# A hybrid diffusion step: three quarters of four output panels move into the last attention group of the grouped-query layers, and GpSimd subtracts in four parts

## The chip, the cores and the metric

The kernel runs on one core of a Trainium2 chip. The metric is the device time of one execution in microseconds (us), the median of several runs. The engines are TensorE (PE, matmuls; PEld its weight loads), VectorE (DVE), ScalarE (ACT), GpSimd (POOL) and SyncE (SP, which here only issues DMA transfers). Each works through a queue of its own in order; semaphores tie them together.

## The reference, cut to what matters

Four layers run over 128 context and 512 latent tokens of width 1024. Layers 0 and 3 are grouped-query attention, layer 1 is differential attention, layer 2 an mLSTM. What the change touches is the end of a grouped-query layer, where the gated attention output is multiplied by `w_out` and added to the residual stream:

```
def gated_out(o, z, w_out):
    return (o.reshape(B, S, -1) * silu(z)) @ w_out

def layer(x, cond):                       # per layer
    shift, scale, gate = adaln(cond, w_mod, b_mod)
    h = rms_norm(x, norm_g) * (1 + scale) + shift
    q, k, v, z = split(h @ w_in)          # 16 query heads, 4 key/value heads
    o = softmax(q k^T / 8) v              # q, k normalised and rotated
    return x + gate * gated_out(o, z, w_out)
```

After layer 3 a last RMSNorm follows. All is float32.

## The kernel before, in words

Activations lie transposed, feature block by token: `x[p, block, token]`, eight blocks of 128 features (`KT`), 640 tokens. A float32 product is made of three passes in a faster format: weights and activations are each split into a high and a low part (`wh`, `wl`; `hh`, `hl` for the layer's input, `yh`, `yl` for the gated attention output), and a matmul unit runs high x high, high x low, low x high. One panel of 128 output features over all tokens is 8 x 3 x 2 = 48 matmuls of 128x128 by 320 tokens.

**Weights.** SP loads a panel of 256 KB into one of three slots of `raw` (in order, each slot when its last reader is done). POOL splits it in `split`: a 128x1 instruction, a cast into `wh`, a subtraction into `wl`, again three slots (`SPL`), each free when PE is done with the panel before. The modulation columns of the next layer (`mod_item`, `mods_at`) use the same `raw` slots; PE reads them directly.

**A grouped-query layer.** `gqa_layer` exists once for each engine. It runs 40 steps: four key/value heads (groups) of ten steps, two query blocks by five token tiles. A step n on PE is: wait for the exponentials of n, values of n - 1, scores of n + 1, transposes of n, and in between a half (320 tokens, 24 matmuls) of one projection panel of this or the next group, taken from a generator in two pieces. `unit_at(n)` says which half; in the last group only two of the ten steps have one (the z gate's second panel, steps 34 and 35). ACT takes exponentials and copies, DVE the maxima, the division and the gating product (`output`). A block b of `yh`, `yl` is complete after five steps: blocks 0 to 5 belong to the first three groups, 6 and 7 to the last.

**The output stretch.** `attention_out` then multiplies the eight panels of `w_out`, 48 matmuls each, into two PSUM accumulators in turn. DVE adds each to `x` with the layer's gate (`add_gated`) and sums its square (`squared`), for the next norm. The last panel (`last_panel`) runs half by half, and the sums of squares go through PE in between. In the last layer `turned_out` also transposes each finished block of `x` back to tokens, after ACT has scaled it; ACT copies the result out (`turned_read`).

The order on every engine is that of the written program; nothing is scheduled at run time.

## Time and profile before

| | |
|---|---|
| median of 3 runs | 2256.95 us (2256.05 to 2260.66) |
| the profiled execution | 2252.97 us, its span 2251.2 us |
| PE busy | 2058.2 us, 91% of the span |
| DVE, ACT, POOL busy | 1177.5, 803.4, 547.6 us (52, 36, 24%) |
| last group and output stretch of layer 3 | 2099.7 to 2175.5, and on to about 2237.6 us |
| last group of layer 0 | 332.7 to 416.2 us |

All times of the sections below are us from the span's start in the one profiled execution. A busy share is a mean over stages with different limits, so the stretches are looked at one by one. The granted clock is the share of TensorE's full speed: 1.00 is 2.4 GHz, 0.5 is 1.2 GHz, and a value between them is a mixture of both in time.

### The profile page before, as it was taken

The page shows a single profiled execution, that of the slowest core. Times are in us where ns is not written, and L with a number is a line of the kernel's source. Part 1 is how long each engine was busy: PE and PEld are TensorE (multiplying, and loading weights), DVE is VectorE, ACT ScalarE, POOL GpSimd, SP SyncE. Part 2 cuts the span into 40 slices and gives each one's busy share as a digit, 9 for nine tenths or more (in the row PEclk, how much of TensorE's full clock was granted, in tenths as well). Part 3 has the DMA queues.
Part 4 walks back from the last instruction along what each step waited for, and adds up shares of the span by engine and source line. Part 5 has one row for each costly group of instructions (what it writes and reads, how often), then busy time and mean ns, then how long its engine had stood idle before and what let it go on. Part 6 is the DMA issues. An engine that isn't in the chain of part 4 may idle for free.

```text
span 2251.2 us, 34991 instructions
## 1 busy us (share of the span) xinstructions
PE 2058.2 (91%) x14168; PEld 1765.2 (78%) x14168; DVE 1177.5 (52%) x2309; ACT 803.4 (36%) x1824; POOL 547.6 (24%) x440
## 2 busy tenths in 40 slices
PE   6999998889999997979979999998997989999888
PEld 4887886878989886968957868687876977888677
DVE  5477665563555553576534323241161666777544
ACT  5365554123444443031132232313221035555432
POOL 1313200433233311334310111102112542222122
PEclk8999998989999998979979999999998989999889
DMA  9212122322223223134222334325236221102001
GB/s 330 56 49 78 51 59 80 89 59 80 66 81 98 63 62 115 38 51 154 81 61 71 91 121 103 94 87 143 93 96 132 68 77 30 51 2 69 20 20 57
DMA packets 302286, 181.53 MB, mean 81 GB/s; under 512 B 59557, under 2 KB 276910, under 8 KB 302126
## 3 DMA queue, kind: packets, MB, share of 16 engines
q1 hardware_dynamic: 283860, 158.39, 24.0%
q10 hardware_dynamic: 18266, 20.90, 4.1%
q8 instruction: 113, 1.85, 0.4%
q14 instruction: 47, 0.39, 0.1%
HBM read 153.51 MB, written 25.74 MB: 80 GB/s over the span
## 4 chain that ended last, share of the span: by engine, by line
PE 75%; DVE 9%; ACT 8%; DMA 3%; issue 3%; SPq 1%; ACTq 1%; POOL 0%; DVEq 0%; POOLq 0%
PE pc L1682 20%; PE acc L1608 12%; PE acc L710 5%; PE acc L1774 4%; PE acc L1763 4%; PE pt L1785 3%; PE acc L700 3%; PE pc L765 3%; PE pt L710 2%; PE acc L1992 2%; PE acc L2004 2%; DMA out_mlstm_n<-amat 1%; PE acc L654 1%; PE pt L2012 1%; PE acc L1938 1%
## 5 line engine op out<-in xcount | busy, mean ns | idle before, releaser
L1523 POOL TENSOR_TENSOR idle<-eps 128x1 f32<-128x1 f32 x144 | 38.1, 264 | 1637.8 <-PE pc L765 306.0
L1682 PE MATMUL pc<-hh,wh 128*128 128x320 f32 x1152 | 380.0, 330 | 16.7 <-DVE hl L2661 8.2
L1526 POOL TENSOR_TENSOR wl<-raw,wh 128x1024 fp32r<-128x1024 f32 x144 | 368.0, 2556 | 11.5
L1682 PE MATMUL pc<-hl,wh 128*128 128x320 f32 x1152 | 362.1, 314 | 0.0
L1682 PE MATMUL pc<-hh,wl 128*128 128x320 f32 x1152 | 361.9, 314 | 0.0
L1682 PEld LDWEIGHTS pc<-hh,wh 128*128 128x128 f32 x1152 | 221.8, 192 | 29.0 <-issue 15.7
L1682 PEld LDWEIGHTS pc<-hl,wh 128*128 128x128 f32 x1152 | 222.8, 193 | 0.2 <-issue 0.2
L1682 PEld LDWEIGHTS pc<-hh,wl 128*128 128x128 f32 x1152 | 221.9, 193 | 0.0
L2283 ACT COPY ht<-pt 128x512 f32<-128x512 f32 (+1 forms) x160 | 76.4, 525 | 214.8 <-PE pt L1785 214.6
L1524 POOL CAST wh<-raw 128x1024 fp32r<-128x1024 f32 x144 | 150.9, 1048 | 0.0
L1774 PE MATMUL acc<-ht,gvt 128*64 128x128 f32 x1344 | 100.7, 298 | 19.3 <-ACT ht L2288 14.9
L1774 PEld LDWEIGHTS acc<-ht,gvt 128*64 128x64 f32 x1344 | 80.2, 148 | 45.6 <-issue 24.7
L2756 DVE TENSOR_REDUCE gst<-acc 128x1 f32<-128x640 f32 (+1 forms) x160 | 113.3, 708 | 3.0 <-PE acc L1763 2.8
L2746 DVE TENSOR_TENSOR gyt<-acc,gzs 128x128 f32<-128x128 f32 x80 | 23.1, 289 | 175.2 <-PE acc L1763 164.0
L2951 DVE SCALAR_TENSOR_TENSOR x<-acc,mod,x 128x128 f32<-128x128 f32 x72 | 36.3, 546 | 139.2 <-PE acc L1608 127.1
L1763 PE MATMUL acc<-gkk,gqf 64*128 64x320 f32 (+1 forms) x576 | 103.3, 476 | 6.1 <-ACT two L2274 6.1
L1608 PE MATMUL acc<-hh,wh 128*128 128x320 f32 x368 | 87.4, 319 | 18.2 <-POOL wl L1526 13.1
L1608 PE MATMUL acc<-yh,wh 128*128 128x320 f32 x400 | 92.1, 311 | 0.0
L1608 PE MATMUL acc<-yl,wh 128*128 128x320 f32 x400 | 91.7, 310 | 0.0
L1608 PE MATMUL acc<-yh,wl 128*128 128x320 f32 x400 | 91.6, 310 | 0.0
L1608 PE MATMUL acc<-hl,wh 128*128 128x320 f32 x368 | 85.7, 315 | 0.0
L1608 PE MATMUL acc<-hh,wl 128*128 128x320 f32 x368 | 85.4, 314 | 0.0
(386 smaller groups left out, 4437.6 us busy)
## 6 DMA issues: line engine op xcount, KB each, us to landing
raw<-in_w_mod SPq DMA_DIRECT2D x144, 256.0 KB, 3.4
raw<-in_gqa_w_in SPq DMA_DIRECT2D x80, 256.0 KB, 3.6
raw<-in_diff_w_in SPq DMA_DIRECT2D x64, 256.0 KB, 3.8
raw<-in_mlstm_w_in SPq DMA_DIRECT2D x64, 256.0 KB, 3.4
praw<-in_w_mod SPq DMA_DIRECT2D x32, 256.0 KB, 9.9
raw<-in_gqa_w_out SPq DMA_DIRECT2D x32, 256.0 KB, 3.2
out_mlstm_C<-amat ACTq DMA_DIRECT2D x16, 512.0 KB, 7.4
raw<-in_mlstm_w_out SPq DMA_DIRECT2D x32, 256.0 KB, 3.1
```

The costliest lines, as they stand in the source:

```text
L700: ins = pe.matmul(acc[b][:, 0:r[1] - r[0]], mk[:, kt, i * P:(i + 1) * P], mq[:, kt, r[0]:r[1]], start=kt == 0, stop=kt == 3)
L710: return pe.matmul(dst, lhsT, rhs, start=start, stop=stop, skip_group_check=True)
L765: ins = pe.matmul(pc[:, c:c + 320], w[:, blk % 2, kt, :], h[:, kt, t:t + 320], start=kt == 0 and n == 0, stop=kt == KT - 1 and n == 2)
L1524: pool.tensor_copy(wh[:, s], raw[:, r]).then_inc(pool_step, 1)
L1526: pool.tensor_tensor(wl[:, s], raw[:, r], wh[:, s].bitcast(F32), ALU.subtract).then_inc(w_full[s], 1)
L1608: ins = pe.matmul(acc[b][:, c:c + 320], w[:, s, kt, :], h[:, kt, t:t + 320], start=kt == 0 and n == 0, stop=kt == KT - 1 and n == 2)
L1682: ins = pe.matmul(pc[:, c:c + 320], w[:, sl, kt, :], h[:, kt, t:t + 320], start=kt == 0 and n == 0, stop=kt == KT - 1 and n == 2)
L1763: ins = pe.matmul(acc[j][:, o:o + c1 - c0], gqf[r, g % 2, blk, q], gkk[r, g % 2, c0:c1], start=True, stop=True)
L1774: ins = pe.matmul(acc[0][HD * j:HD * j + HD, 0:P], gvt[:, g % 2, t, :], ht[:, j, i * P:(i + 1) * P], start=i == 0, stop=t == tiles[-1], sk ...
L1785: ins = pe.transpose(pt[:, 512 * j + i * P:512 * j + (i + 1) * P], gee[n % 2][:, j, i * P:(i + 1) * P], ident)
L2283: act.copy(ht[:, j, 0:w], pt[:, 512 * j:512 * j + w]).then_inc(pts_dve, 1)
L2756: step(dve.tensor_reduce(gst[:, p, j:j + 1], acc[j][:, AO:AO + w], AX.X, ALU.max, negate=True))
```

## The change

- `unit_at`: in the last group the z gate's second panel moves from steps 34, 35 to steps 30, 31.
- `early_at`, `early_mms`: steps 32 to 39 each take half of one of the output panels 0 to 3, but only over the six row blocks that exist by then (`EARLY_KT`): 18 matmuls into `pc`, in two pieces of 9. DVE adds the half to `x` one step later (`early_gated`).
- `attention_out`: panel 4 comes first, then one panel of weights that holds the last two row blocks for panels 0 to 3, 12 matmuls each, then panels 5, 6, 7. In the last layer the transposes follow that order, three in a row behind panel 5 and two behind panel 6.
- SP and POOL load and split the panels in that order. A grouped-query layer now has nine panels of output weights instead of eight, so the slots of layer 1 begin elsewhere (`FIRST_SLOT`).
- `split`: the subtraction is made in four instructions of 256 elements instead of one of 1024, for all 144 (now 146) splits of the kernel.

```diff
@@ -389,9 +390,23 @@
         def unit_at(n):
 
             g, s = n // NS2, n % NS2
+            if g == GQ_KV - 1:
+                return ("z1", g, s) if s < 2 else None
             kind = KINDS[s // 2]
             grp = g + (kind != "z1")
             return (kind, grp, s % 2) if grp < GQ_KV else None
+
+        def early_at(n):
+
+            s = n - (GQ_KV - 1) * NS2 - 2
+            return (s // 2, s % 2) if s >= 0 else None
+
+        def out_slots(kind, layer):
+
+            s = FIRST_SLOT[layer] + PANELS[kind]
+            if kind == "diff":
+                return [((s + i) % SPL, (i,)) for i in range(KT)]
+            return [((s + EARLY + i) % SPL, panels) for i, panels in enumerate(GQ_OUT)]
 
         def mods_at(n, layer):
...
@@ -409,7 +424,10 @@
 
         FIRST = ("kv", "q0", "q1", "z0")
         PANELS = {"gqa": 5 * GQ_KV, "diff": 4 * NH}
-        FIRST_SLOT = (0, 1, 0, 2)
+        FIRST_SLOT = (0, 2, 0, 2)
+        EARLY, EARLY_KT = 4, 6
+        GQ_OUT = ((4,), (0, 1, 2, 3), (5,), (6,), (7,))
+        LAST_ORDER = [i for panels in GQ_OUT for i in panels]
 
         def totals(kind, layer):
...
@@ -1449,8 +1467,16 @@
                             item(at[0], at[1])
                             if at[0] == "q0":
                                 cache(at[1])
-                        if n >= NN - 2:
-                            whole(ring(), wo, (n - NN + 2) * P, [w_full[wring()]] * RAW)
+                        early = early_at(n)
+                        if early is not None and early[1] == 0:
+                            whole(ring(), wo, early[0] * P, [w_full[wring()]] * RAW)
+                        if n == NN - 2:
+                            whole(ring(), wo, EARLY * P, [w_full[wring()]] * RAW)
+                        if n == NN - 1:
+                            slot = ring()
+                            panel(slot, [(raw[:, slot, 4 * k:4 * k + 4, :],
+                                          wo[(EARLY_KT + k) * P:(EARLY_KT + k + 1) * P, 0:EARLY * P].rearrange("p (i c) -> p i c", c=P))
+                                         for k in range(2)], [w_full[wring()]] * RAW)
                         for m in mods_at(n, layer):
                             mod_item(m)
...
@@ -1523,8 +1549,10 @@
                 pool.tensor_tensor(idle[:, :], eps[:, 0:1], eps[:, 0:1], ALU.add)
                 pool.tensor_copy(wh[:, s], raw[:, r]).then_inc(pool_step, 1)
                 pool.wait_ge(*seen(pool_step))
-                pool.tensor_tensor(wl[:, s], raw[:, r], wh[:, s].bitcast(F32), ALU.subtract).then_inc(w_full[s], 1)
-                seen.lend(("w", s), done[s])
+                for k in range(0, KT, 2):
+                    ins = pool.tensor_tensor(wl[:, s, k:k + 2], raw[:, r, k:k + 2], wh[:, s, k:k + 2].bitcast(F32), ALU.subtract)
+                ins.then_inc(w_full[s], 1)
+                seen.lend(("w", s), done[s], times)
 
             pool.wait_ge(x_in, QT)
...
@@ -1546,8 +1574,11 @@
                         at = unit_at(n)
                         if at is not None and at[2] == 0:
                             split(ring(), wring(), units)
+                        early = early_at(n)
+                        if early is not None and early[1] == 0:
+                            split(ring(), wring(), [early_done] * SPL, 2)
                         if n >= NN - 2:
-                            split(ring(), wring())
+                            split(ring(), wring(), proj_done, 1 if n == NN - 2 else EARLY)
                         for m in mods_at(n, layer):
                             mod_item()
...
@@ -1697,6 +1728,36 @@
 
                 seen(raw_full[ring()], 32)
                 outs_open.append(wring())
+
+            def early_mms(half):
+
+                sl, (t, c) = early_slot[0], HALF[half]
+                seen.back(pe, ("c", half))
+                for kt in range(EARLY_KT):
+                    for n, (w, y) in enumerate(((wh, yh), (wh, yl), (wl, yh))):
+                        ins = pe.matmul(pc[:, c:c + 320], w[:, sl, kt, :], y[:, kt, t:t + 320],
+                                        start=kt == 0 and n == 0, stop=kt == EARLY_KT - 1 and n == 2)
+                        if kt == EARLY_KT // 2 - 1 and n == 2:
+                            yield
+                ins.then_inc(early_done, 1)
+                seen.lend(("c", half), early_added)
+
+            def early_panel(n, gen):
+
+                early = early_at(n)
+                if early is None:
+                    return None
+                if gen is None:
+                    if early[1] == 0:
+                        seen(raw_full[ring()], 32)
+                        early_slot[0] = wring()
+                        pe.wait_ge(*seen(w_full[early_slot[0]]))
+                        pe.wait_ge(*seen.at(y_ready, EARLY_KT))
+                    gen = early_mms(early[1])
+                    next(gen)
+                    return gen
+                for _ in gen:
+                    pass
 
             def mod_sum(m, at):
...
@@ -1885,10 +1946,11 @@
                     if n + 1 < NN:
                         scores(n + 1)
                     turn_p(n)
-                    gen = part(n, None)
+                    gen, early = part(n, None), early_panel(n, None)
                     if n % QT:
                         turn_fifth(n)
                     part(n, gen) if gen else None
+                    early_panel(n, early) if early else None
                     if st == 1:
                         rotate_q("q1", g)
...
@@ -1924,7 +1986,8 @@
                 seen.end(totals(kinds[layer], layer))
                 if turn.k % 2 == 0:
                     turn()
-                for i in range(2, KT):
+                final = layer + 1 == DEPTH
+                for i in range(2 if kinds[layer] == "diff" else EARLY + 1, KT):
                     out_panel()
                 first = outs_open[0]
                 pe.wait_ge(*seen(w_full[first]))
-                    pe.wait_ge(fin_full, kt + 1)
-                    if kt >= 2:
-                        pe.wait_ge(fin_read, kt - 1)
+                if kinds[layer] == "diff":
+                    for sl in outs_open[1:-1]:
+                        project(sl, yh, yl, freed_by=x_ready)
+                    last_panel(outs_open[-1], yh, yl)
+                    outs_open.clear()
+                    return
+
+                def turned_out(p):
+
+                    dst = (pt, pc)[p % 2]
+                    pe.wait_ge(fin_full, p + 1)
+                    if p >= 2:
+                        pe.wait_ge(fin_read, p - 1)
                     for q in range(QT):
-                        ins = pe.transpose(dst[:, q * P:(q + 1) * P], ht[:, kt % 2, q * P:(q + 1) * P], ident)
+                        ins = pe.transpose(dst[:, q * P:(q + 1) * P], ht[:, p % 2, q * P:(q + 1) * P], ident)
                     ins.then_inc(fin_turned, 1)
 
-                final = layer + 1 == DEPTH
-                for i, sl in enumerate(outs_open[1:-1]):
+                for half in range(2):
+                    seen.back(pe, ("c", half))
+                rest = outs_open[1]
+                pe.wait_ge(*seen(w_full[rest]))
+                for i in range(EARLY):
+                    b = buffer(x_ready)
+                    for kt in range(KT - EARLY_KT):
+                        for n, (w, y) in enumerate(((wh, yh), (wh, yl), (wl, yh))):
+                            for t, c in halves():
+                                ins = pe.matmul(acc[b][:, c:c + 320], w[:, rest, 4 * kt + i, :], y[:, EARLY_KT + kt, t:t + 320],
+                                                start=kt == 0 and n == 0, stop=kt == KT - EARLY_KT - 1 and n == 2)
+                    ins.then_inc(proj_done[rest], 1)
+                if final:
+                    turned_out(0)
+                for k, sl in enumerate(outs_open[2:-1]):
                     project(sl, yh, yl, freed_by=x_ready)
                     if final:
-                        turned_out(i)
+                        for p in ((1, 2, 3), (4, 5))[k]:
+                            turned_out(p)
                 bs = last_panel(outs_open[-1], yh, yl, final)
...
@@ -2703,6 +2788,15 @@
                     dve.wait_ge(*seen(zt_ready))
                     dve.scalar_tensor_tensor(out=gzs[:, int(kind == "z1"), t:t + 320], in0=gzt[:, t:t + 320], scalar=1.0, in1=pc[:, c:c + 320],
                                              op0=ALU.add, op1=ALU.mult).then_inc(c_free[half], 1)
+
+                def early_gated(i, half):
+
+                    (t, c), mod = HALF[half], mods[layer % 2]
+                    dve.wait_ge(*seen(early_done))
+                    for a0, a1, g in (((0, P, 0), (P, 320, 1)), ((0, 320, 1),))[half]:
+                        ins = dve.scalar_tensor_tensor(out=x[:, i, t + a0:t + a1], in0=pc[:, c + a0:c + a1], scalar=mod[:, 2 * KT + i, g:g + 1],
+                                                       in1=x[:, i, t + a0:t + a1], op0=ALU.mult, op1=ALU.add)
+                    ins.then_inc(early_added, 1)
 
                 def k_reciprocal(j):
...
@@ -2799,7 +2893,11 @@
                         output(n - 1)
                     at = unit_at(n - 1) if n else None
                     if at is not None and at[0] in ("z0", "z1"):
+                        if not more and at[0] == "z1":
+                            dve.wait_ge(*seen.at(o_ready, NS2 * g))
                         gate(*at)
+                    if n and early_at(n - 1) is not None:
+                        early_gated(*early_at(n - 1))
                     if st == 1 and g:
                         y_low(2 * g - 1)
                     if st == 2:
@@ -2826,6 +2924,7 @@
                 if layer + 1 < DEPTH:
                     modulation(layer + 1)
                 y_low(NN // QT - 1)
+                early_gated(*early_at(NN - 1))
                 seen.end(totals("gqa", layer))
                 if turn.k % 2 == 0:
...
@@ -2999,11 +3098,17 @@
                 else:
                     diff_layer()
 
-                for i in range(KT - 1):
-                    add_gated((FIRST_SLOT[layer] + PANELS[kind] + i) % SPL, i, layer)
-                    dve.wait_ge(*seen(x_ready))
-                    squared(i)
-                last_gated((FIRST_SLOT[layer] + PANELS[kind] + KT - 1) % SPL, layer)
+                if kind == "gqa":
+                    dve.wait_ge(*seen(early_added, 2 * EARLY))
+                outs, p = out_slots(kind, layer), 0
+                for s, panels in outs[:-1]:
+                    for i in panels:
+                        add_gated(s, i, layer)
+                    for i in panels:
+                        dve.wait_ge(*seen(x_ready))
+                        squared(i, p)
+                        p += 1
+                last_gated(outs[-1][0], layer)
             use()
             dve.wait_ge(*seen(root_ready))
```

PE in the last group of layer 3, from the values matmuls behind the short tile on (`ht`, `gvt`: values; `gkk`, `gqf`: scores; `two`, `gee`: transposes of the probabilities; `yh`, `yl`, `wh`, `wl`: output panels). Before:

```order
L1774 MATMUL acc<-ht,gvt 64x128 x2
L1763 MATMUL acc<-gkk,gqf 128x320 x4
L1785 MATMUL pt<-consts,two 128x128 x8
L1794 MATMUL pt<-consts,two 128x128 x2
L1774 MATMUL acc<-ht,gvt 64x128 x10
```

And of the change, up to the first three of the 18 early matmuls of that step:

```order
L1835 MATMUL acc<-ht,gvt 64x128 x2
L1824 MATMUL acc<-gkk,gqf 128x320 x4
L1846 MATMUL pt<-consts,two 128x128 x8
L1738 MATMUL pc<-yh,wh 128x320
L1738 MATMUL pc<-yl,wh 128x320
L1738 MATMUL pc<-yh,wl 128x320
```

Where the step had only attention, nine output matmuls now stand ahead of the fifth tile's transposes and nine behind them.

SP's queue in the last group of layer 0 (`in_w_mod`: modulation columns, two rows for each; `in_gqa_w_out`: output panels, two rows each). Before:

```order
L1384 DMA raw<-in_gqa_w_in 128x4x128 x2
L1384 DMA raw<-in_w_mod 128x4x128 x12
L1384 DMA raw<-in_gqa_w_out 128x4x128 x2
L1384 DMA raw<-in_w_mod 128x4x128 x2
L1384 DMA raw<-in_gqa_w_out 128x4x128 x2
L1384 DMA raw<-in_w_mod 128x4x128 x2
L1384 DMA raw<-in_gqa_w_out 128x4x128 x12
```

And of the change, from the second pair of columns of the group on:

```order
L1402 DMA raw<-in_w_mod 128x4x128 x4
L1402 DMA raw<-in_gqa_w_out 128x4x128 x2
L1402 DMA raw<-in_w_mod 128x4x128 x4
L1402 DMA raw<-in_gqa_w_out 128x4x128 x2
L1402 DMA raw<-in_w_mod 128x4x128 x4
L1402 DMA raw<-in_gqa_w_out 128x4x128 x2
L1402 DMA raw<-in_w_mod 128x4x128 x8
L1402 DMA raw<-in_gqa_w_out 128x4x128 x4
L1402 DMA raw<-in_w_mod 128x4x128 x2
L1402 DMA raw<-in_gqa_w_out 128x512 x2
L1402 DMA raw<-in_w_mod 128x4x128 x2
L1402 DMA raw<-in_gqa_w_out 128x4x128 x6
```

Output panels now stand between the columns instead of behind nearly all of them, and the row of 128x512 is the panel of the last two row blocks.

DVE in one step of the last group of layer 3 (`gst`: maxima and their scaling, `gee`: the division, `yl`: low part of a finished block). Before:

```order
L2746 TENSOR_TENSOR gyt<-acc,gzs 128x128
L2756 TENSOR_REDUCE gst<-acc 128x1
L2757 TENSOR_TENSOR gst<-gst,grq 128x1
L2691 TENSOR_TENSOR yl<-gyt,yh 128x640
L2765 RECIPROCAL gst<-gst 128x1
L2766 SCALAR_TENSOR_TENSOR gee<-gee,gst,half_col 128x640
```

And of the change:

```order
L2840 TENSOR_TENSOR gyt<-acc,gzs 128x128
L2850 TENSOR_REDUCE gst<-acc 128x1
L2851 TENSOR_TENSOR gst<-gst,grq 128x1
L2797 SCALAR_TENSOR_TENSOR x<-pc,mod,x 128x320
L2776 TENSOR_TENSOR yl<-gyt,yh 128x640
L2859 RECIPROCAL gst<-gst 128x1
```

The addition of an early half (`x<-pc,mod,x`) stands behind the step's maxima and ahead of the division.

## Rows read from the trace of the kernel before

**Rows 1.** The page, busy us of each engine, share of the span, instructions.

```profile
PE 2058.2 (91%) x14168; PEld 1765.2 (78%) x14168; DVE 1177.5 (52%) x2309; ACT 803.4 (36%) x1824; POOL 547.6 (24%) x440
```

**Rows 2.** Busy time by stretch: third and last groups of layers 0 and 3.

```profile
core 0: us, PE busy (x) PEld busy (x) DVE busy (x) ACT busy (x) POOL busy (x), PEclk, DMA share, GB/s
253.10:332.70 79.60, 78.13 (x678) 65.99 (x674) 56.91 (x110) 44.85 (x104) 14.85 (x12) 1.00 0.22 62
332.70:416.20 83.50, 65.77 (x602) 49.96 (x598) 44.00 (x91) 35.45 (x83) 12.81 (x11) 0.82 0.33 95
2024.00:2099.70 75.70, 74.57 (x601) 63.34 (x600) 55.89 (x110) 44.08 (x100) 20.75 (x15) 1.00 0.20 59
2099.70:2175.50 75.80, 56.92 (x381) 41.73 (x381) 40.55 (x91) 32.76 (x72) 7.40 (x6) 0.80 0.05 15
```

**Rows 3.** The chain that ended last, layer 3's output stretch: start, us, what.

```profile
2191.11 0.55 PE pt L1948 x5
2191.65 7.05 PE acc L1608 x48
```

**Rows 4.** DVE's timeline in that stretch, additions: start, us, instruction, idle before.

```profile
2184.10 1.01 DVE L2951 SCALAR_TENSOR_TENSOR x<-acc,mod,x 128x128 f32<-128x128 f32 x2 [5.33 <-PE acc L1938]
...
2233.17 0.68 DVE L2977 SCALAR_TENSOR_TENSOR x<-acc,mod,x 128x128 f32<-128x128 f32 x2 [1.27 <-PE acc L1636]
```

**Rows 5.** ACT's timeline in that stretch, the scaling of one block.

```profile
2230.21 0.83 ACT L2521 ACTIVATE ht<-x,cols 128x640 f32<-128x640 f32 x1 [6.18 <-DVE x L2951]
```

**Rows 6.** Busy time by step: 20, 21, 22, 24, 28 and 29 of layer 3.

```profile
2024.00:2030.40 6.40, 6.40 (x55) 5.45 (x54) 3.61 (x10) 3.37 (x8) 0.00 (x0) 1.00 0.41 111
2030.40:2038.00 7.60, 7.48 (x49) 5.75 (x48) 6.45 (x11) 4.74 (x12) 4.60 (x5) 1.00 0.67 196
2038.00:2047.50 9.50, 9.50 (x77) 7.96 (x76) 6.94 (x13) 5.12 (x10) 3.19 (x2) 1.00 0.19 57
...
2055.40:2063.70 8.30, 8.28 (x70) 7.51 (x70) 8.09 (x14) 4.68 (x11) 4.23 (x3) 1.00 0.22 65
...
2086.00:2093.30 7.30, 7.30 (x64) 6.32 (x63) 5.35 (x11) 4.71 (x10) 4.00 (x3) 1.00 0.24 72
2093.30:2099.70 6.40, 6.40 (x59) 5.93 (x58) 3.03 (x11) 2.77 (x8) 0.00 (x0) 1.00 0.01 3
```

**Rows 7.** PE's timeline, step 22 of layer 3: the key sums.

```profile
2046.35 1.29 PE L1807 MATMUL pt<-gsk,consts 64*64 64x320 f32 x4
```

**Rows 8.** ACT's timeline, steps 32 and 33 of layer 3.

```profile
2121.70 1.28 ACT L2301 ACT_TABLE_LOAD   x1
...
2126.64 1.07 ACT L2283 COPY ht<-pt 128x512 f32<-128x512 f32 x2 [3.37 <-PE pt L1785]
```

**Rows 9.** Timeline of a step at clock 1.00 (35 of layer 3): PE, then ACT.

```profile
2140.19 1.31 PE L1774 MATMUL acc<-ht,gvt 128*64 128x128 f32 x20
2141.44 1.35 PE L1763 MATMUL acc<-gkk,gqf 64*128 64x320 f32 x8
...
2144.99 0.88 ACT L2274 ACTIVATE two<-acc,gst,grq 128x640 f32<-128x640 f32 x1
```

**Rows 10.** SP's and POOL's timeline in layer 0, from a panel's issue to its split.

```profile
391.04 1.06 SPq L1384 DMA_DIRECT2D raw<-in_gqa_w_out  x2
...
395.55 0.19 POOL L1523 TENSOR_TENSOR idle<-eps 128x1 f32<-128x1 f32 x1 [45.67 <-DMA raw<-in_gqa_w_out]
...
396.80 2.36 POOL L1526 TENSOR_TENSOR wl<-raw,wh 128x1024 fp32r<-128x1024 f32 x1
```

**Rows 11.** Timeline of POOL, DVE and PE: layer 3's step 24, layer 0's output stretch.

```profile
2056.86 2.85 POOL L1526 TENSOR_TENSOR wl<-raw,wh 128x1024 fp32r<-128x1024 f32 x1
2057.89 1.84 DVE L2757 TENSOR_TENSOR gst<-gst,grq 128x1 f32<-128x1 f32 x1
...
469.23 2.88 DVE L2962 TENSOR_TENSOR two<-two 128x640 f32<-128x640 f32 x1
...
472.26 1.04 PE L1650 MATMUL acc<-two,consts 128*128 128x320 f32 x3 [1.54 <-DVE two L2962]
```

**Rows 12.** The page's groups: matmuls of the mLSTM's output, idle before and releaser.

```profile
L1608 PE MATMUL acc<-hh,wh 128*128 128x320 f32 x368 | 87.4, 319 | 18.2 <-POOL wl L1526 13.1
```

44 lines of the change are left out of this document (22 added, 22 removed).

## The prediction

> **What bounds the kernel now.** The page comes first: TensorE (PE) is busy for 91% of the span and no other engine is near it [rows 1], so time is won by taking PE's instructions off the path, by filling PE's idle time, or by raising its clock. The second view is the busy time by stretch. It shows a difference inside the attention of a grouped-query layer. An ordinary group of ten steps (steps 20 to 29; ten steps per key/value head) takes 79.6 us in layer 0 and 75.7 us in layer 3, PE busy for 78.1 and 74.6 us, granted clock 1.00. The last group (steps 30 to 39) has 192 fewer projection matmuls and takes 83.5 and 75.8 us: PE is busy for only 65.8 and 56.9 us, and the granted clock is 0.82 and 0.80 [rows 2]. A clock of 0.80 between the levels 2.4 and 1.2 GHz means 40% of the stretch at the lower one. So the last group does less and takes as long: it idles, and the idling brings slow matmuls. Third, the chain that ended last: right behind that group stand eight output panels, 48 matmuls each, 7.05 us per panel with nothing between them but 0.55 us of transposes in the last layer [rows 3]. That stretch is pure PE. The change moves work from the full stretch into the hollow one.
>
> **The output stretch.** Of panels 0 to 3, six of eight row blocks go into steps 32 to 39: 4 x 36 = 144 matmuls per layer. The rest, 4 x 12, costs what one panel did. At 7.05/48 = 0.147 us a matmul [rows 3] the stretch loses 21.1 us, for two layers **-42.2**.
>
> The four short accumulations of the rest panel (12 x 0.147 = 1.76 us each) alternate between two accumulators, and each wants VectorE's (DVE's) addition of the one two back: one takes 1.01 us [rows 4], so DVE keeps up. Four squares are queued behind these additions instead of between them. They have one panel of PE time (7 us) and are needed two panels later; nothing waits. In the last layer three transposed panels stand in a row behind panel 5, through two buffers. The third waits for ScalarE (ACT) to copy out the first (about as long as its scaling of one panel, 0.83 us [rows 5]) and to scale the next: 0.55 + 0.8 + 0.8 - 1.1 = **+1.0**, once.
>
> **The last group.** What one step costs I read from ordinary steps with their 24 projection matmuls, all at clock 1.00 [rows 6], and take off what is missing: 6 x 0.147 = 0.88 us where 18 early matmuls stand for 24.
> - 30 and 31 (the z1 panel moved here): 6.4 and 7.6, as steps 20 and 21.
> - 32: step 22 (9.5) less the next head's key sums (1.2 [rows 7]) less 0.88: 7.4.
> - 33: ACT loads a table and takes one root while PE still works on values (1.25), scores (1.3) and half of the transposes (0.4); then it copies (1.07), loads the other table (1.28) and takes two exponentials (1.9): 6.9, with the semaphores between some 7.2 [rows 8, 9]. PE, with 6.4, waits here.
> - 34: step 29 (6.4) less 0.88: 5.5.
> - 35: PE would need 5.5, but from the start of the values matmuls over scores and maxima to the end of the second exponential, which the next step waits for, are 5.7 (2140.19 to 2145.87) [rows 9]: the floor of any full step.
> - 36: step 28 (7.3) less 0.88, less 16 of 20 values matmuls (1.0): 5.4.
> - 37, 38: 7.3 - 0.88 = 6.4 each. 39: without scores (1.3), 5.1.
>
> Sum 63.1. DVE gets the additions of the early halves, 0.68 us where a half has two pieces and less where it has one [rows 4], behind its maxima, while ACT takes exponentials; the transposes want DVE's result only 2.5 us (values and scores) into the next step, so PE's other matmuls hide them. Six weight splits of GpSimd (POOL) fall in this group and can hold up DVE inside the floor chain: +1.0. Layer 3: 64.1 against 75.8, **-11.7**. The bounds: 63 below, and above the 75.7 of an ordinary group, if something other than PE sets the length of its steps. I take the lower end because PE was busy for 74.6 of those 75.7 us.
>
> Layer 0 also has 12 sums of modulation columns in this group. Four of them lengthen its ordinary group by 79.6 - 75.7 = 3.9 us, so 0.98 each: 63.1 + 1.0 + 11.7 = 75.8. Here the transfer queue (SP's) matters: early panels and columns share three landing slots, and SP issues in order. From an issue to POOL's start are 4.5 us, from there to the subtraction 1.25, the subtraction takes 2.36 and its added parts 0.6: together 8.7 [rows 10]. Panel 3 gets its slot when the second column of step 36 has been copied, about 1.8 us into step 37 counting the issue ahead of it, and is ready at 10.5; PE wants it at 7.4 + 3.4 = 10.8. Column 23 follows the split of panel 4: ready 0.4 + 8.7 + 4.5 = 13.6 us into step 38, wanted at 7.4 + 5.2. I allow 1.5: 77.3 against 83.5, **-6.2**. In layer 3 there are no columns and weights come two steps early.
>
> **The subtraction in parts.** A DVE instruction that reads SBUF twice can stand still until POOL's subtraction ends: a product of two 128x1 columns took 1.84 us and ended at 2059.73, the subtraction beside it at 2059.71. In layer 0's output stretch a sum of squares took 2.88 in that way, and PE waited 1.54 us for it [rows 11]. A quarter of 2.36 is 0.6, and that wait shrinks to some 0.4: **-1.1**. Elsewhere PE's idle time in the six ordinary groups is about 1.1 to 1.5 each, 8 in all [rows 2], half of it the table loads of step 23; I take **-2.0**, bounds 0 and -4. The price: three more instructions per split, at most 0.19 each, what a 128x1 one takes [rows 10]. It is hidden wherever weights are early; in the mLSTM's output stretch PE waited 13.1 us for one split [rows 12], so **+0.6** there.
>
> The Trainium skill (GPSIMD Engine Reference, section 3.1 Elementwise) speaks against parts: each instruction pays two software dispatch hops and a join of eight cores. Its 4497 ns for 2048 elements at 2.6 cycles leave, as an estimate, 0.06 us for that, or +0.2 for my +0.6.
>
> **Sum.** -42.2 + 1.0 - 11.7 - 6.2 - 1.1 - 2.0 + 0.6 = -61.6. The durations are those of the profiled execution, 2252.97 us (span 2251.2), which becomes 2191.4; it lies 4.0 below the median of the runs, so against 2256.95 I forecast **2195**.
>
> **Rivals.**
> *The last group keeps an ordinary group's length.* If the additions on DVE, or stalls behind POOL, hold each step at what it took with 24 matmuls, the groups take 75.7 and 79.6 + 8 x 0.98 = 87.4: +3.8 in place of -17.9, so -39.9, **2217**. For it: DVE is busy for 8.1 of 8.3 us in step 24, and POOL splits more often here. Against it: that step's length was PE's, and the last group has no rotation or key scaling for a next head. Chance 0.17.
>
> *Weights late in layer 0.* If panels 3, 4 and the rest each come a whole 8.7 us late, 26 us go again: **2221**. For it: three slots, an in-order queue, and a margin of 0.3 us worked out above. Against it: the lateness would have to add up from panel to panel, while each step leaves 7 us. Chance 0.07.
>
> *The clock falls in the last group: slower.* Place: steps 32 to 39. Their PE work at the upper level is some 47 us per layer and doubles at the lower: +94 for both layers against -61.6 gives +32, **2289**. It decides from two thirds of those steps at 1.2 GHz on. For it: this very group ran 40% of its time there. Against it: it idled 19 of 76 us, and the ordinary groups of [rows 2] have 1.00 at 98% busy; the new steps idle only in 33 and 35, about 1 us. The Trainium skill (TensorE: Matmul & The Clock Gate, section A second HAM failure mode: psum-queue depth-cycling) has such a case: matmul groups that rotate through PSUM banks leave short idle times, and the clock swings. Ordinary steps rotate through the same two halves of pc each step and show no fall, so here row and rule differ. Chance 0.03.
>
> **How the numbers follow.** The forecast, with its unknowns (group sums within 6, parts from 0 to -4, lateness 0 to 5), holds 2184 to 2206 and has 0.73. A measurement tells 0.2% (4.5 us) from no change. The range goes down to 2183 and up over the first rival's value to **2218**, which leaves out about 0.05 below and 0.1 above. Only the clock case is on the other side: faster 0.96, same 0.01, slower 0.03.
>
> **What would show it.** Right: the last groups at 62 to 67 and 73 to 80 us with clock near 1.00; the output stretch from the last values to the end of the last panel shorter by 21 us per layer; one PE wait of 1 us before the third transposed panel; DVE's slowest 128x1 product under 0.9 us. Wrong: PE idle in steps 34 to 38 with DVE as the releaser (first rival), PE waiting for wl or raw in layer 0 (second), clock 0.5 in steps 32 to 39 (third).

## The result and the profile after

The changed kernel takes **2180.09 us** (median of 4 runs, 2179.51 to 2181.97) beside 2258.71 us (2256.05 to 2260.66) for the kernel before on the same chip: a ratio of 0.9657, 95% interval 0.9643 to 0.9671. The forecast was 2195 us and its range began at 2183: the direction was right, but the gain, 78 us, is larger than forecast, and the time lies 2.9 us under the range.

The page's busy time, the line that answers to [rows 1]:

```profile
PE 2021.1 (93%) x14168; PEld 1742.8 (80%) x14168; DVE 1114.4 (51%) x2333; ACT 803.8 (37%) x1824; POOL 653.9 (30%) x884
```

PE has as many matmuls as before and needs 37 us less for them. POOL is busy for 106 us more, and DVE, with 24 instructions more, for 63 us less. Nothing in the change takes work from DVE. So DVE records must contain time in which the instruction stood still, and that time fell.

The last groups, by stretch (layer 0, then layer 3), which answer to the second and fourth row of [rows 2]:

```profile
core 0: us, PE busy (x) PEld busy (x) DVE busy (x) ACT busy (x) POOL busy (x), PEclk, DMA share, GB/s
333.97:409.84 75.87, 72.19 (x748) 61.02 (x740) 47.77 (x102) 35.58 (x84) 27.05 (x37) 1.00 0.44 126
2057.78:2122.63 64.85, 62.70 (x526) 53.24 (x524) 45.92 (x102) 32.77 (x72) 22.69 (x30) 1.00 0.14 42
```

83.5 became 75.9 and 75.8 became 64.9, with more matmuls in them and the clock at 1.00 instead of 0.82 and 0.80. The same view by step, layer 3, steps 30 to 39 in order:

```profile
2057.78:2064.18 6.40, 6.40 (x56) 5.45 (x54) 3.57 (x8) 2.84 (x8) 3.98 (x6) 1.00 0.14 40
2064.18:2071.44 7.26, 7.26 (x50) 5.73 (x48) 6.42 (x14) 4.41 (x10) 0.53 (x2) 1.00 0.14 39
2071.44:2078.85 7.41, 7.41 (x67) 6.54 (x66) 5.24 (x11) 4.07 (x8) 3.71 (x5) 1.00 0.25 73
2078.85:2086.70 7.85, 6.59 (x58) 5.54 (x57) 4.97 (x13) 5.03 (x10) 1.11 (x2) 1.00 0.00 0
2086.70:2092.27 5.57, 5.46 (x52) 5.10 (x52) 4.60 (x13) 2.34 (x7) 3.90 (x5) 1.00 0.06 18
2092.27:2098.10 5.83, 5.70 (x50) 4.58 (x48) 3.00 (x9) 2.29 (x7) 0.00 (x0) 1.00 0.26 75
2098.10:2104.43 6.33, 5.79 (x40) 4.55 (x40) 6.19 (x11) 4.05 (x9) 4.91 (x6) 1.00 0.02 7
2104.43:2110.87 6.44, 6.33 (x56) 5.48 (x56) 4.71 (x13) 3.08 (x7) 0.00 (x0) 1.00 0.26 77
2110.87:2117.35 6.48, 6.48 (x58) 5.48 (x56) 4.62 (x12) 3.12 (x7) 4.55 (x6) 1.00 0.04 13
2117.35:2122.63 5.28, 5.28 (x49) 4.78 (x48) 2.62 (x6) 1.53 (x3) 0.00 (x0) 1.00 0.30 86
```

The forecast for these steps was 6.4, 7.6, 7.4, 7.2, 5.5, 5.7, 5.4, 6.4, 6.4, 5.1. It missed step 33 by 0.65 and step 36 by 0.9 us; in step 36 PE stood still for 0.54 us, DVE was busy for 6.19 of the 6.33 us and POOL was splitting for 4.91.

PE's timeline in the output stretch of layer 3, the transposes behind panel 5:

```profile
2145.75 0.71 PE L2018 MATMUL pc<-consts,ht 128*128 128x128 f32 x5
2146.30 0.71 PE L2018 MATMUL pt<-consts,ht 128*128 128x128 f32 x5
2147.97 0.77 PE L2018 MATMUL pc<-consts,ht 128*128 128x128 f32 x5 [0.96 <-ACT ht L2606]
```

The third one waits 0.96 us for ACT; 1.0 was forecast.

The instruction whose stall [rows 11] showed, all 160 of it in the kernel before and in the changed one (shortest, median and longest in ns):

```profile
L2757 DVE TENSOR_TENSOR gst<-gst,grq x160: 158/159/2315, 91.7 to 2168.1; 128x1 f32<-128x1 f32 x160
L2851 DVE TENSOR_TENSOR gst<-gst,grq x160: 159/160/750, 95.0 to 2115.9; 128x1 f32<-128x1 f32 x160
```

The longest is 0.75 us, under the 0.9 forecast. Before, it was 2.32 us; the one that [rows 11] showed, 1.84 us, was not the longest.

### The profile page after: what moved, and what is told of

The parts are those of the page before. It is cut to its first block, busy times and chain, and to the rows that moved or that the text cites. A ratio compares the mean times of both kernels' runs of the same rounds, so it can differ in the third digit from the quotient of the medians.

```text
span 2178.5 us, 35475 instructions
## 1 busy us (share of the span) xinstructions
PE 2021.1 (93%) x14168; PEld 1742.8 (80%) x14168; DVE 1114.4 (51%) x2333; ACT 803.8 (37%) x1824; POOL 653.9 (30%) x884
## 4 chain that ended last, share of the span: by engine, by line
PE 77%; DVE 8%; ACT 7%; DMA 4%; issue 2%; SPq 1%; ACTq 1%; POOL 0%; DVEq 0%; POOLq 0%
PE pc L1713 21%; PE acc L1639 10%; PE acc L728 6%; PE acc L1835 4%; PE acc L1824 4%; PE pc L783 3%; PE acc L718 3%; PE pt L1846 3%; PE pt L728 3%; PE acc L2076 2%; PE acc L2088 2%; DMA out_mlstm_n<-amat 1%; PE acc L672 1%; PE acc L1667 1%; PE pt L2096 1%
## 5 line engine op out<-in xcount | busy, mean ns | idle before, releaser
L1549 POOL TENSOR_TENSOR idle<-eps 128x1 f32<-128x1 f32 x146 | 43.5, 298 | 1458.8 <-PE pc L783 297.5
L1553 POOL TENSOR_TENSOR wl<-raw,wh 128x256 fp32r<-128x256 f32 x584 | 467.2, 831 | 11.7
L1713 PE MATMUL pc<-hh,wh 128*128 128x320 f32 x1152 | 381.0, 331 | 15.8 <-DVE hl L2743 7.7
L1639 PE MATMUL acc<-hh,wh 128*128 128x320 f32 x368 | 86.9, 318 | 18.7 <-POOL wl L1553 13.2
L1824 PE MATMUL acc<-gkk,gqf 64*128 64x320 f32 (+1 forms) x576 | 95.4, 445 | 4.7 <-ACT two L2358 4.7
L1835 PE MATMUL acc<-ht,gvt 128*64 128x128 f32 x1344 | 91.0, 278 | 3.8 <-ACT ht L2372 3.4
L1835 PEld LDWEIGHTS acc<-ht,gvt 128*64 128x64 f32 x1344 | 71.9, 136 | 28.1 <-issue 22.4
L783 PE MATMUL pc<-hh,wh 128*128 128x320 f32 x256 | 81.2, 317 | 1.0 <-issue 0.7
L728 PE MATMUL acc<-mv,amat 128*128 128x256 f32 (+1 forms) x344 | 80.7, 380 | 0.0
L1639 PEld LDWEIGHTS acc<-hh,wh 128*128 128x128 f32 x368 | 62.7, 192 | 20.8 <-issue 13.4
```

What stands on the lines that cost most here:

```text
L728: return pe.matmul(dst, lhsT, rhs, start=start, stop=stop, skip_group_check=True)
L783: ins = pe.matmul(pc[:, c:c + 320], w[:, blk % 2, kt, :], h[:, kt, t:t + 320], start=kt == 0 and n == 0, stop=kt == KT - 1 and n == 2)
L1553: ins = pool.tensor_tensor(wl[:, s, k:k + 2], raw[:, r, k:k + 2], wh[:, s, k:k + 2].bitcast(F32), ALU.subtract)
L1639: ins = pe.matmul(acc[b][:, c:c + 320], w[:, s, kt, :], h[:, kt, t:t + 320], start=kt == 0 and n == 0, stop=kt == KT - 1 and n == 2)
L1713: ins = pe.matmul(pc[:, c:c + 320], w[:, sl, kt, :], h[:, kt, t:t + 320], start=kt == 0 and n == 0, stop=kt == KT - 1 and n == 2)
L1824: ins = pe.matmul(acc[j][:, o:o + c1 - c0], gqf[r, g % 2, blk, q], gkk[r, g % 2, c0:c1], start=True, stop=True)
```

## Where the time went, stretch by stretch

Lengths in us, from the start of one matmul to the start of another in each kernel's profiled execution: a grouped-query layer's groups from the values matmuls of step 0 to those of 29 and of 39; its output from there to the first matmul of the last panel; the convolution from the first gate matmul of the mLSTM to the end of its last convolution addition on DVE. The columns in the middle are experiments told below.

| stretch | before | before + 4 parts | changed, 1 part | changed | changed, again |
|---|---|---|---|---|---|
| start, to layer 0's values | 99.4 | 99.7 | 100.4 | 104.3 | 98.0 |
| layer 0, groups 0 to 2 | 233.3 | 229.3 | 233.6 | 229.8 | 229.6 |
| layer 0, last group | 83.5 | 82.4 | 78.4 | 75.9 | 75.4 |
| layer 0, output | 50.85 | 50.85 | 29.96 | 29.74 | 29.74 |
| layer 0, last panel | 9.75 | 8.11 | 12.40 | 8.19 | 8.16 |
| mLSTM, convolution | 174.5 | 170.0 | 173.0 | 167.5 | 167.5 |
| mLSTM, what follows to its last panel | 673.3 | 676.8 | 680.2 | 670.2 | 680.9 |
| ahead of layer 3 | 61.8 | 59.5 | 61.8 | 59.6 | 59.4 |
| layer 3, groups 0 to 2 | 220.3 | 219.6 | 220.4 | 219.6 | 219.6 |
| layer 3, last group | 75.8 | 72.0 | 67.1 | 64.9 | 64.8 |
| layer 3, output | 53.85 | 53.84 | 33.89 | 33.89 | 33.88 |

Three things are in it. The outputs are shorter by 21.1 and 20.0 us and the last groups by 7.6 and 10.9, near the forecast. The parts gain in stretches that the forecast gave nothing or little. And two stretches, the start and the mLSTM behind its convolution, differ by 6.3 and 10.7 us between two executions of the same changed kernel; a difference in them says nothing about the change. Layer 0's last group also varies: in two other profiles whose layer 0 is the kernel before it took 79.8 and 85.5 us, so its 7.6 us could as well be 4 or 10. Layer 3's took 75.4 to 75.8 us in the same three profiles.

## The experiments

The theory after the result: what was mis-sized is the subtraction in parts. By this theory, any DVE instruction that reads SBUF twice stands still for one GpSimd instruction on a panel, so stalls shrink with the length of that instruction, in every stretch where DVE is on the path. The rival: the parts are worth the 2.5 us of the forecast, and the rest came from the slots or from the filled steps.

### The parts alone, the early panels alone, the slots alone

Before with the four parts (shortened):

```diff
-wl[:, s], raw[:, r], wh[:, s] in one subtraction
+for k in range(0, KT, 2): wl[:, s, k:k + 2], raw[:, r, k:k + 2], wh[:, s, k:k + 2]
```

> The kernel before with the subtraction in four parts and nothing else. If the parts are what shortened the mLSTM layer (theory): that layer about 10 us shorter than before between the end of layer 1 and its own last panel, ordinary groups of the grouped-query layers 4 us shorter together, norms and tails 4 us; ratio to before 0.991 to 0.994 (14 to 20 us). If the shifted weight slots did it (rival): the mLSTM layer as before, ratio 0.996 to 0.999.

The changed kernel with the subtraction whole (the same edit backwards):

> The changed kernel with the subtraction whole again; early panels, moved z gate and order of the output kept. Theory: the moved panels alone give 53 to 59 us as the terms of the prediction have it (output stretches 41 us, last groups 11 and 7): 2195 to 2205 us, mLSTM layer as long as before. Rival (slots): mLSTM layer still 10 us shorter, 2185 us or less.

Before with the slots of the change:

```diff
-        FIRST_SLOT = (0, 1, 0, 2)
+        FIRST_SLOT = (0, 2, 0, 2)
```

> The kernel before with the slots of layer 1, and so those that the mLSTM layer finds free first, shifted as in the changed kernel, and nothing else. Theory: within 0.1% of before. Rival: 8 to 10 us shorter, all of it in the mLSTM layer.

| kernel | median us (range) | ratio to before, 95% interval |
|---|---|---|
| before + 4 parts | 2241.54 (2239.51 to 2244.35) | 0.9922 (0.9904 to 0.9940) |
| changed, subtraction whole | 2210.44 (2208.55 to 2212.04) | 0.9780 (0.9765 to 0.9795) |
| before, other slots | 2260.3 (2254.95 to 2266.66) | 1.0001 (0.9986 to 1.0015) |

The parts alone bring 17.7 us (0.0078 x 2261.6), not 2.5. The rest of the change alone brings 49.8 us, less than the 53 to 59 expected. On top of it the parts bring some 28 us more by the two ratios (0.9780 and 0.9657), or 25 with the changed kernel run again (0.9667, below). The slots make no difference that can be told from none (interval 3 us either way). The rival is out. One expectation failed: with the parts alone the mLSTM layer was to be 10 us shorter; its convolution is 4.5 us shorter, but what follows is 3.5 us longer, which is within what that stretch varies by.

### Which length counts

The changed kernel with the subtraction in two and in eight instructions:

```diff
-                for k in range(0, KT, 2):    # 256 elements each
+                for k in range(0, KT, 4):    # the first kernel: 512
+                for k in range(0, KT, 1):    # the second: 128
```

> The changed kernel with the subtraction in two instructions of 512 elements instead of four. With one instruction it took 2210.4 us, with four 2180.1 us. Theory (what is saved goes with the length of one instruction, which other engines must sit out: 2.56 us whole, 0.83 us as a quarter, some 1.4 us as a half): two thirds of the 30 us come back at once, 2188 to 2193 us. Rival (only the breaking up as such counts, a wait of 1.4 us is as harmless as one of 0.8): 2178 to 2183 us.

> The changed kernel with the subtraction in eight instructions of 128 elements. Theory (length of one instruction, here some 0.5 us): another 5 us, 2173 to 2177 us. Rival (each further instruction costs GpSimd about 0.25 us, as the step from one to four did, 2.56 to 3.32 us per split, and where TensorE waits for the split that shows): 2181 to 2186 us.

| parts | mean of one, us | all subtractions, POOL us | DVE busy, us | median us (range) |
|---|---|---|---|---|
| 1 | 2.55 | 372 | 1193.6 | 2210.44 (2208.55 to 2212.04) |
| 2 | 1.41 | 407 | 1150.1 | 2189.87 (2188.37 to 2190.57) |
| 4 | 0.83 | 467 | 1114.4 | 2180.09 (2179.51 to 2181.97) |
| 8 | 0.53 | 574 | 1084.5 | 2177.51 (2172.86 to 2183.31) |

Two parts came out at 2189.9 inside the theory's 2188 to 2193. From one part to four POOL is busy for 95 us more and DVE for 79 us less, and down to four parts the time follows the length of one instruction. At eight the range of the runs covers both sides: a gain of 2.6 us is not told from none, and the ratios to before are the same (0.9657 and 0.9661). The rule does not hold in every place. With one, two, four and eight parts the convolution takes 173.0, 170.6, 167.5 and 166.9 us, but the last panel of layer 0 takes 12.4, 12.5, 8.2 and 8.5: there halves are no better than the whole.

### Where the stalls are

Parts in the mLSTM layer alone, then in layers 0 and 3 alone, on the kernel before (shortened):

```diff
+            def split(r, s=None, done=proj_done, parts=1):    # 4 from mlstm_pool
+            parts = 4 if kind == "gqa" else 1                 # the second kernel
```

> The kernel before with the subtraction in four parts in the mLSTM layer alone (48 of 144 splits). In all layers it brought 17.7 us. Theory (VectorE's column additions in the mLSTM's convolution are the path there, and stand still for a whole subtraction): 5 to 9 us of it are here, 2252 to 2257 us, the four heads' convolution phase about 169 us instead of 174.5. Rival 1 (all of it is won in the attention layers, what the mLSTM shows is the spread of its transfers): 2260 to 2263 us. Rival 2 (all of it is here): 2242 to 2246 us.

> The kernel before with the subtraction in four parts in layers 0 and 3 alone. In all layers it brought 17.7 us, in the mLSTM layer alone 5 to 7. Theory (the grouped-query layers hold the rest: steps that stand still for a subtraction and then run at a lower granted clock, the last panel of layer 0, the last groups): 10 to 13 us, 2246 to 2249 us, and no step of layer 0's ordinary groups above 9.7 us. Rival (the forecast was right here, 2.0 + 1.1 us, and the rest is in the differential layer): 2254 to 2257 us.

The mLSTM alone: 2251.41 us (2248.53 to 2258.93), ratio 0.9977 (0.9960 to 0.9994), some 5 us, with a convolution of 170.0 us. Layers 0 and 3 alone: 2244.29 us (2232.97 to 2249.85), ratio 0.9933 (0.9908 to 0.9959), some 15 us. No step of layer 0's ordinary groups is above 9.7 us there any more. The first gain is at the low end of the 5 to 9 us expected, the second above its 10 to 13. The two add up to the 17.7 within their intervals, so nothing points to the differential layer, which was not tried alone. The convolution took 172.1 to 174.6 us in the five profiles that have the subtraction whole there, and 167.5 to 170.0 in the five with four parts and the cast whole. With parts only in layers 0 and 3, the last panel of layer 0 stays at 9.75 us: the subtraction beside it is that of a panel of layer 1.

Three places show how a stall becomes PE's time. First the last panel of layer 0, POOL, DVE and PE in the changed kernel with the subtraction whole:

```profile
433.18 0.82 DVE L3058 TENSOR_TENSOR two<-x 128x640 f32<-128x640 f32 x1
435.71 1.03 POOL L1550 CAST wh<-raw 128x1024 fp32r<-128x1024 f32 x1
435.75 1.67 DVE L3059 TENSOR_TENSOR two<-two 128x640 f32<-128x640 f32 x1
436.83 2.87 POOL L1552 TENSOR_TENSOR wl<-raw,wh 128x1024 fp32r<-128x1024 f32 x1
437.46 2.92 DVE L3058 TENSOR_TENSOR two<-x 128x640 f32<-128x640 f32 x1
...
444.25 2.83 POOL L1552 TENSOR_TENSOR wl<-raw,wh 128x1024 fp32r<-128x1024 f32 x1
444.89 1.01 DVE L3048 SCALAR_TENSOR_TENSOR x<-acc,mod,x 128x128 f32<-128x128 f32 x2
...
448.78 2.47 PE L1679 MATMUL acc<-two,consts 128*128 128x320 f32 x4 [2.64 <-DVE two L3059]
```

and in the changed kernel:

```profile
434.86 4.46 POOL L1553 TENSOR_TENSOR wl<-raw,wh 128x256 fp32r<-128x256 f32 x4
435.49 1.25 DVE L3061 TENSOR_TENSOR two<-two 128x640 f32<-128x640 f32 x1
...
443.34 1.31 PE L1681 MATMUL acc<-two,consts 128*128 128x320 f32 x4
```

A square takes 0.82 us by itself, 2.92 beside the whole subtraction and 1.25 beside a quarter. The addition that reads PSUM and `x` is not held up (1.01 us beside a subtraction, as in [rows 4]). PE waits 2.64 us for the sum of squares, or not at all.

The mLSTM's convolution, DVE and POOL, with the subtraction whole:

```profile
993.01 5.59 DVE L1168 SCALAR_TENSOR_TENSOR cv<-r,cols,cv 128x642 f32<-128x642 f32 x3
995.03 2.87 POOL L1552 TENSOR_TENSOR wl<-raw,wh 128x1024 fp32r<-128x1024 f32 x1
```

and in the changed kernel:

```profile
984.09 3.94 DVE L1168 SCALAR_TENSOR_TENSOR cv<-r,cols,cv 128x642 f32<-128x642 f32 x3
986.14 4.73 POOL L1553 TENSOR_TENSOR wl<-raw,wh 128x256 fp32r<-128x256 f32 x4
```

Three additions take 1.65 us less; the phase repeats such places for each of four heads and is 4.5 to 7 us shorter with parts.

The third goes through the clock. Steps 2 and 3 of layer 0, first with the subtraction whole (the run with other slots), then in the changed kernel:

```profile
109.20:120.51 11.31, 10.69 (x78) 8.15 (x76) 7.70 (x12) 5.92 (x12) 5.37 (x4) 0.90 0.01 1
120.51:131.13 10.62, 10.21 (x82) 8.16 (x82) 5.77 (x11) 5.87 (x13) 0.00 (x0) 0.78 0.00 0
```

```profile
111.88:121.40 9.52, 9.52 (x77) 7.97 (x76) 7.07 (x12) 5.29 (x11) 7.53 (x10) 1.00 0.01 3
121.40:129.73 8.33, 7.93 (x79) 6.70 (x78) 5.43 (x10) 6.21 (x14) 0.00 (x0) 1.00 0.00 0
```

In the first pair, this is what happened in step 2: the subtraction, the product of two columns that stands still, and ACT, which waits for it:

```profile
112.24 2.40 POOL L1526 TENSOR_TENSOR wl<-raw,wh 128x1024 fp32r<-128x1024 f32 x1
112.66 2.00 DVE L2757 TENSOR_TENSOR gst<-gst,grq 128x1 f32<-128x1 f32 x1
...
114.69 0.89 ACT L2274 ACTIVATE gee<-acc,gst,grq 128x640 f32<-128x640 f32 x1 [1.43 <-DVE gst L2757]
```

PE idled 0.6 us later in that step (the profile names no releaser, so that this stall is the reason is argued from the order). The granted clock was 0.90 over that step and 0.78 over the next, and the two steps together took 4.1 us longer. In the profile of the kernel before, step 13, behind such a stall, ran at 0.83 and took 9.9 us instead of 8.3; in four others with the subtraction whole it was step 3 or 23 or both. With four parts, steps 2, 12 and 22 take 9.5 us and steps 3, 13 and 23 8.33 in every profile. So in layer 0 the parts save the stall and the slow matmuls behind it, together 4 to 7 us in the ordinary groups. Not every such stall is followed by slow matmuls (step 12 of the same run was not), and what decides it was not tried.

### What made the last group short

> The changed kernel, with only two of the six row blocks multiplied in steps 32 to 39 (6 matmuls a step instead of 18); four row blocks of panels 0 to 3 are left out of the output. Theory (the last group was long because PE idled and its clock fell): with less to do the last group of layer 3 is no shorter than the 64.9 us of the changed kernel, granted clock 0.8 to 0.9, group 66 to 74 us. Rival (the clock does not matter, only PE's own work and the chain of maxima and exponentials): 96 matmuls less make it 55 to 60 us.

```diff
-                for kt in range(EARLY_KT):
+                for kt in range(2):
...
```

This kernel leaves out four of six row blocks of the early panels and was run once. Steps 33 and 35 of layer 3, then its whole last group:

```profile
2085.84:2093.69 7.85, 4.74 (x46) 3.68 (x47) 5.92 (x15) 5.84 (x10) 2.94 (x5) 1.00 0.00 1
2098.42:2104.65 6.23, 3.84 (x38) 2.82 (x39) 3.71 (x10) 2.49 (x7) 2.22 (x4) 1.00 0.08 25
...
2065.73:2127.91 62.18, 50.23 (x431) 40.21 (x431) 45.31 (x102) 32.34 (x72) 23.50 (x31) 0.97 0.14 43
```

62.2 us, between what the theory and the rival expected, so neither is right as put. Twelve of 18 matmuls less shorten the group by only 2.7 us (step 33 not at all): the steps stand near a floor, which the prediction took for the chain from values over maxima to exponentials. Step 33 stays at 7.85 us, as the ordinary step 23 with 24 matmuls does. With 6 matmuls per step the granted clock was 0.97, where the old group had 0.80. The full 18 therefore cost almost nothing there. In layer 0 the same kernel's last group even took 77.3 us at a clock of 0.96, longer than the 75.9 with all 18.

Then one move of the change alone, on the kernel before:

```diff
+            if g == GQ_KV - 1:
+                return ("z1", g, s) if s < 2 else None
...
+                        if not more and at[0] == "z1":
+                            dve.wait_ge(*seen.at(o_ready, NS2 * g))
```

> The kernel before with one thing of the change: the second panel of the z gate in the last group stands in its first two steps instead of its fifth and sixth. No early panels, the subtraction whole. Theory (the last group is short in the changed kernel because its steps are filled and the clock stays up): the empty steps leave the granted clock below 0.9, the last groups keep 70 us or more in layer 3 and 78 or more in layer 0, the time is within 6 us of before, 2255 to 2262. Rival (the last groups were long because of where the z gate's panel stood): 62 to 67 us in layer 3, and 2238 to 2248 us in all.

The last groups of layers 0 and 3:

```profile
336.04:422.08 86.04, 69.90 (x600) 52.57 (x599) 43.33 (x91) 35.42 (x84) 9.66 (x9) 0.76 0.32 93
2107.77:2174.70 66.93, 49.91 (x382) 37.73 (x382) 39.35 (x91) 32.34 (x72) 7.33 (x6) 0.88 0.06 17
```

2248.57 us (2241.41 to 2254.72), ratio 0.9961 (0.9943 to 0.9980): some 9 us are gained, more than the theory allowed and just less than the rival's 10 to 20. In layer 3 the rival is right about the group: 66.9 us, at a clock of 0.88, without one early panel; 1.9 us of it go again, since the output stretch then begins slowly (55.74 us instead of 53.85). In layer 0 the group stays at 86.0 us with the clock at 0.76, as the theory has it. Steps 31 and 34 of layer 3 show what the move does, first in the kernel before, then with the panel moved:

```profile
2105.56:2114.66 9.10, 6.73 (x24) 3.37 (x25) 6.10 (x13) 3.63 (x8) 0.00 (x0) 0.71 0.11 32
2131.27:2140.20 8.93, 8.93 (x59) 8.18 (x60) 2.83 (x10) 2.44 (x7) 0.00 (x0) 0.70 0.00 0
...
2114.17:2121.43 7.26, 7.26 (x51) 5.74 (x51) 5.79 (x13) 3.90 (x9) 0.81 (x2) 1.00 0.02 5
2137.19:2143.44 6.25, 4.70 (x37) 3.72 (x36) 2.66 (x10) 2.32 (x7) 0.00 (x0) 0.73 0.00 0
```

Before, the panel's first half stood in step 34, behind hollow steps, and PE worked it off at a granted clock of 0.70; moved, it follows full steps, and step 31 runs at 1.00. In the changed kernel with the subtraction whole, both groups have a clock of 1.00 too:

```profile
333.88:412.27 78.39, 72.17 (x748) 61.03 (x740) 51.54 (x102) 35.45 (x84) 22.74 (x20) 1.00 0.45 129
2083.89:2150.95 67.06, 62.91 (x526) 53.22 (x524) 47.56 (x102) 33.07 (x72) 19.89 (x15) 1.00 0.13 40
```

So in layer 3 the group's gain without the parts is that of the moved panel (66.9 and 67.1 us); what the early panels add there is the work from the output stretch at no cost in steps, and in layer 0 the clock.

### A faster version

The cast in two, alone and with eight parts, and the changed kernel again beside them (the edit of the cast):

```diff
-                pool.tensor_copy(wh[:, s], raw[:, r]).then_inc(pool_step, 1)
+                for k in range(0, KT, 4):
+                    ins = pool.tensor_copy(wh[:, s, k:k + 4], raw[:, r, k:k + 4])
+                ins.then_inc(pool_step, 1)
```

> The changed kernel with the cast ahead of the subtraction in two instructions as well (1.05 us whole, then some 0.55 each). Theory (VectorE stands still for any GpSimd instruction on whole panels, so now the cast is the longest): 32 VectorE instructions lie mostly beside a cast and are 21 us longer than the shortest of their kind; half of that goes, a quarter of it on the path: 2176 to 2178.5 us. Rival (the stalls come from the subtraction alone, whatever lies beside the cast): 2179 to 2183 us, 0.25 us more of GpSimd per split.

> The changed kernel with the cast in two and the subtraction in eight instructions. Eight parts alone took 2177.5 us. Theory (length of one instruction): the two gains add, 2172 to 2177 us. Rival (the price of further instructions on GpSimd, 4.5 us of busy time per split instead of 3.3, eats it): 2179 to 2185 us.

> The changed kernel once more, unaltered, beside the two others. Both theories: 2178 to 2183 us; the profiled execution shows how far the mLSTM layer and the start alone differ from one execution of the same program to the next, expected 3 to 6 us, and every step of the grouped-query layers within 0.5 us of the first profile.

| kernel | median us (range) | ratio to before, 95% interval |
|---|---|---|
| changed, again | 2185.73 (2178.05 to 2188.96) | 0.9667 (0.9641 to 0.9692) |
| cast in two | 2180.19 (2174.03 to 2186.85) | 0.9649 (0.9622 to 0.9677) |
| cast in two, 8 parts | 2173.68 (2169.01 to 2175.79) | 0.9621 (0.9597 to 0.9645) |

In the profile the cast in two shortens the ordinary groups of layers 0 and 3 by 1.2 and 1.3 us (228.4 and 218.3), in the time it is not told from nothing: the median lies in the rival's range, the runs spread over both. With eight parts the median lies in the theory's range, and it is faster than the changed kernel run beside it: their ranges don't meet. It has the lowest time of the kernels run, but against eight parts with the cast whole (0.9661, 0.9635 to 0.9687) the intervals overlap, so what the cast adds is open. The changed kernel itself came out above its expected 2178 to 2183, 5.6 us higher than in its first runs, with a range of 10.9 us; all its grouped-query steps agree with the first profile within 0.5 us, and what differs is the start and the mLSTM's later part. The 2.9 us by which the result lay under the forecast's range are within that spread; that the parts were worth ten times their term is not.

## Why the prediction missed, and which step failed

**Output stretches** (-42.2, and +1.0 for the third transposes): right. 21.1 and 20.0 us, a wait of 0.96.

**Last groups** (-11.7 and -6.2): near in size, 10.9 and 7.6, at clock 1.00. That filling keeps the clock up is borne out: 1.00 even with the subtraction whole. But in layer 3 the move of the z gate's panel does most of it. And the size holds only with the parts: whole, the subtraction leaves the groups at 67.1 and 78.4.

**Layer 0's tail** (-1.1): 1.6. But the sentence that four squares are queued and nothing waits is wrong by itself: with the subtraction whole they come late and the last panel takes 12.4 us instead of 9.75. Four parts hide it.

**The subtraction in parts** (-2.0 with bounds 0 and -4, beside -1.1 for the tail and +0.6): this step failed. The mechanism was right, an instruction on VectorE that stands still beside the whole subtraction. Its price was read from PE's idle time in the six ordinary groups, and together the three terms gave 2.5 us; the parts were worth 17.7 us alone and 25 to 28 on top of the moved panels. It left out three things. The first is the stretches outside these groups where DVE is on the path: the convolution 4.5 us, the stretch ahead of layer 3 2.3, layer 3's last group of before 3.8 (layer 0's varies too much from one execution to the next to tell). The second is that PE's idle time is not the whole price of a stall, since matmuls behind it can run at a lower clock (with the stalls themselves 4 us in layer 0's groups, from 233.3). The third is that the share of the stalls in those groups differs from one execution to the next: 233.3 in the profile that was read, 233.6 to 236.5 in four others with the subtraction whole.

The price of the parts themselves was forecast about right per split: from the shortest whole subtraction, 2.34 us, and the shortest quarter, 0.72, three more instructions cost 0.53 us, where three times 0.19 was forecast. The Trainium skill (GPSIMD Engine Reference, section 3.1 Elementwise) has each instruction pay its dispatch, and the trace agrees that they pay; the 0.06 us for one that the prediction estimated from that page is low against 0.18 for each further instruction here. But the 0.6 us did not show where it was forecast: PE's wait for the split in the mLSTM's output was 13.1 us before, 13.7 in the changed kernel with the subtraction whole, and 13.2 with the parts.

**The sum.** Two errors partly cancel. The moves alone brought 49.8 us where the forecast had 59.1, since with the subtraction whole the groups and layer 0's last panel are longer than it reckoned; the parts on top brought ten times their 2.5 us. That the result lies only 2.9 us outside the range is in part luck. By stretch, moves and parts together: -21.1 - 20.0 - 7.6 - 10.9 = -59.6 in the outputs and last groups, and elsewhere layer 0's groups -3.5, its last panel -1.6, ahead of layer 3 -2.2, layer 3's groups -0.7 and the convolution -7.0, in all -74.6. The two profiled executions differ by 72.7 us and the medians by 76.9 to 78.6. What is left is of the size by which the start and the mLSTM's later part vary, and stays unassigned.

**The rivals.** None of the three happened. The last groups did not keep an ordinary group's length (64.9 us, not 75.7), though step 33 kept its 7.85 us; no panel was late enough to show in the length of layer 0's group, and the clock did not fall.

## What to carry to other kernels

Where GpSimd and VectorE work beside each other on SBUF, try to cut GpSimd's long instructions into pieces: in this kernel the length of one counted for the others more than the sum, down to quarters, where a further piece cost GpSimd 0.18 us. Price a stall by comparing VectorE's records of one shape (the longest against the shortest) all over the program, not by PE's idle time in the stretch one happens to read, and add the matmuls behind it that run at the lower clock. And when a hollow stretch is filled, ask first for its floor: up to there the filling was nearly free here.

## What was not expected of the hardware

GpSimd and VectorE hold each other up in both directions: four quarters take 4.46 us beside squares, 2.87 (4 x 0.718) at their shortest, and a square 1.25 instead of 0.82. The cast, which reads one operand, holds a square up too (one that began with it took 1.67 us, in the rows above). The Trainium skill (SBUF — State Buffer, section SBUF: two separate sides) describes this as a lock that whoever starts first keeps for its whole instruction, against VectorE instructions with two SBUF inputs; the squares at 2.92 us and the unhindered additions from PSUM agree. In one run a step in which PE idled once for 0.6 us had a granted clock of 0.90 and the next one 0.78, while the group with 6 early matmuls per step, in which PE idled 12 of 62 us, kept 0.97.
